# Shifting the tokens of a short convolution: two DMAs of 127 rows in place of four of 112 and 15

## The reference

```python
def short_conv_mixer(x_in, b_g, c_g, p):
    u = c_g * x_in
    up = jnp.pad(u, ((0, 0), (1, 1), (0, 0)))
    w = p['conv_w']
    y = up[:, :-2] * w[0] + up[:, 1:-1] * w[1] + up[:, 2:] * w[2] + p['conv_b']
    return b_g * y

x = x + gate1 * (jnp.concatenate([o_a, o_b, o_c, o_d], axis=-1) @ p['w_out'])
```

## Time and profile before

| | before |
|---|---|
| median of 3 runs | 5456.26 us (5455.68 to 5457.26) |
| the profiled execution | 5455.68 us, its span 5453.9 us |
| busy share of the span | PE 60%, DVE 69%, POOL 51%, PEld 32%, ACT 12% |
| hardware DMA queue (SyncE's) | 69332 packets, 7.3% of the 16 DMA engines |
| software DMA queue (the experts) | 368640 packets, 62.2% |

### The profile page before, as it was taken

How to read it: one execution, slowest core, us unless ns; L and a number is a source line. 1 busy time by engine, 2 the same in 40 slices (tenths; PEclk the granted TensorE clock), 3 DMA queues, 4 the chain that set the end, 5 groups by cost and what they waited for, 6 DMA issues and landing times. The chain is left out here.

```text
span 5453.9 us, 39401 instructions
## 1 busy us (share of the span) xinstructions
PE 3258.3 (60%) x12134; PEld 1731.0 (32%) x12134; DVE 3782.4 (69%) x7387; ACT 657.4 (12%) x1592; POOL 2758.7 (51%) x2848
## 2 busy tenths in 40 slices
PE   7988888893507145071479787699470541705326
PEld 1467725551202011020134676465220110202102
DVE  1046565379798897988630565736989979799784
ACT  0012122111101000010110121311010100101001
POOL 0012230157777777777730222303677777777775
PEclk9989988997859678595799899699795875958769
DMA  7100042199999999999961000007999999999999
GB/s 265 51 4 2 1 151 68 70 351 397 410 409 404 409 399 408 403 404 409 402 261 51 5 1 18 16 32 258 397 409 410 405 408 397 409 409 398 409 402 365
DMA packets 438180, 1483.20 MB, mean 272 GB/s; under 512 B 47514, under 2 KB 54802, under 8 KB 436306
## 3 DMA queue, kind: packets, MB, share of 16 engines
q0 software_dynamic: 368640, 1342.34, 62.2%
q1 hardware_dynamic: 69332, 138.35, 7.3%
HBM read 1466.17 MB, written 11.73 MB: 271 GB/s over the span
## 5 line engine op out<-in xcount | busy, mean ns | idle before, releaser
L1741 PE MATMUL ps<-z,o 128*128 128x512 f32 x2560 | 1261.4, 621 | 705.2 <-DMA z<-in_peer_v,experts 353.2
L1773 DVE CUSTOM_DVE_ANT_0 z<-z,ps 128x1024 f32<-128x1024 f32 x1280 | 1530.3, 1216 | 64.5 <-DMA z<-in_peer_u,experts 26.7
L1596 POOL DMA_INDIRECT z<-in_peer_u,experts x1280 | 1211.4, 946 | 569.0 <-DVE state L1773 252.1
L1596 POOL DMA_INDIRECT z<-in_peer_v,experts x1280 | 1211.0, 946 | 464.1 <-issue 303.4
L1798 DVE SCALAR_TENSOR_TENSOR ps<-z,state,ps 128x1024 f32<-128x1024 f32 x630 | 808.4, 1283 | 395.7 <-DMA z<-in_peer_v,experts 395.1
L1741 PEld LDWEIGHTS ps<-z,o 128*128 128x128 f32 x2560 | 451.3, 194 | 1510.4 <-ACT o L1654 931.7
L1669 PE MATMUL ps<-const,hT 128*128 128x128 f32 x80 | 17.8, 396 | 1163.2 <-ACT o L1654 1163.2
L1669 PEld LDWEIGHTS ps<-const,hT 128*128 128x128 f32 x80 | 14.4, 207 | 1168.5 <-ACT o L1654 1014.8
L1654 ACT ACTIVATE o<-const,state 128x128 f32<-128x128 f32 x640 | 244.3, 398 | 1068.2 <-PE ps L1741 1063.6
L431 PE MATMUL ps<-w,hT 128*128 128x512 f32 (+1 forms) x960 | 365.6, 543 | 1.8 <-DVE hT L401 1.8
L679 POOL TENSOR_TENSOR kn<-kn,neg_half 128x4 f32<-128x4 f32 x20 | 20.1, 1007 | 482.8 <-DVE kn L717 399.5
(11 more groups left out here) (363 smaller groups left out, 4682.6 us busy)
## 6 DMA issues: line engine op xcount, KB each, us to landing
w<-in_w_mod SPq DMA_DIRECT2D x12, 2048.0 KB, 8.0
gate<-in_w_mod SPq DMA_DIRECT2D x96, 256.0 KB, 3.0
w<-in_w_in SPq DMA_DIRECT2D x10, 2048.0 KB, 8.0
z<-in_peer_u,experts POOLq DMA_INDIRECT x1280, 13.4
z<-in_peer_v,experts POOLq DMA_INDIRECT x1280, 12.1
w<-in_peer_wq SPq DMA_DIRECT2D x8, 2048.0 KB, 12.6
w<-in_w_out SPq DMA_DIRECT2D x4, 2048.0 KB, 11.3
scores<-rows SPq DMA_DIRECT2D x8, 1024.0 KB, 8.8
```

What stands on the lines that cost most here:

```text
L1596: eng.indirect_dma_start(m.ring[j % RING], None, at_layer_rows(table), bass.IndirectOffsetOnAxis(ap=m.experts[:, t % 2, k:k + 1], axis=0)) ...
L1741: mm = eng.matmul(m.ps[:, 4 + n, :], m.diag[:, (done + q) % DIAGS, :], row_j[:, n * 512:(n + 1) * 512], start=(q == 0), stop=(q == SLOTS / ...
L1773: eng.tensor_tensor_reduce(row_j, row_j, h_rows, 1.0, 0.0, ALU.mult, ALU.add, m.acts[:, k:k + 1]).then_inc(used_v, 1)
```

## The change

Each shift is one DMA of 127 rows where there were two, of 112 and of 15. The two small ones stay. The order on SyncE changes a little, and the waits count four DMAs and not six.

```diff
-                for a, b in ((0, 112), (112, P - 1)):
-                    eng.dma_start(before[a + 1:b + 1, :, :], u[a:b, :, :]).then_inc(shifted, 16)
-                    eng.dma_start(after[a:b, :, :], u[a + 1:b + 1, :, :]).then_inc(shifted, 16)
+                eng.dma_start(before[1:P, :, :], u[0:P - 1, :, :]).then_inc(shifted, 16)
                 eng.dma_start(before[0:1, 2:TILES, :], u[P - 1:P, 1:TILES - 1, :]).then_inc(shifted, 16)
+                eng.dma_start(after[0:P - 1, :, :], u[1:P, :, :]).then_inc(shifted, 16)
                 eng.dma_start(after[P - 1:P, 1:TILES - 1, :], u[0:1, 2:TILES, :]).then_inc(shifted, 16)
...
-                eng.wait_ge(shifted, 96)
+                eng.wait_ge(shifted, 64)
...
-                        eng.wait_ge(shifted, 96)
+                        eng.wait_ge(shifted, 64)
```

## The result

The changed kernel takes 5526.09 us (median of 4 runs, 5523.89 to 5530.31) beside 5456.76 us for the one before (4 runs, 5455.68 to 5457.94): 69.3 us or 1.3% slower, ratio 1.0131, 95% interval 1.0118 to 1.0142. The spans are 5522.6 and 5453.9 us, 68.7 apart. The forecast was 5539 with a range of 5515 to 5608.

A forecast was written before the change was run, and what follows sets the result against it. Most of the span was put in the expert stages, at 400 to 410 GB/s, with the shifts hidden. Delays of 38.2 (second layer) and 45.3 us (first) make 83.5; 5455.7 + 83.5 = 5539 us, range 5515 to 5608.

The forecast's parts named there:

- One engine for 127 rows: Shifts: engines get equal shares, so 127 rows run on one; the other reading, rows counted up to 16, gives 16.
- 48 ns a piece, 61.0 us: Shifts: 1270 pieces of 1 KB through one engine at 48 ns each take 61.0 us, against about 6 before.
- Second layer, a wait at GpSimd less 5.6 us of slack: GpSimd's first convolution instruction waits 43.9 us; idle time before the keys' root absorbs 5.6, leaving 38.2 us.
- First layer, the wait at TensorE's piece 4, nothing at GpSimd: Weight loads queue behind the shifts, so TensorE waits 43.3 us for piece 4; GpSimd then finds its data there.
- The clock, 2 us: First layer: after idling, TensorE's work behind the stall may restart at clock 0.50; 0 to 5 us, taken as 2.
- First layer, 45.3 us: First layer's whole cost: TensorE's wait of 43.3 us for piece 4 plus 2 us for the clock.
- The sum, 83.5: Whole kernel: 38.2 us for the second layer plus 45.3 for the first, 83.5 us slower.
- All 16 engines: Rival: 127 rows spread over 16 engines in shares of 7 and 8, still hidden; 5455.5 us, chance 0.07.
- One slow engine: Rival: a lone engine also takes 74 ns a piece, so the transfer takes 94.5 us; 5606 us, chance 0.15.
- Loads not held back: Rival: the engine turns to weight loads between pieces, first layer pays at GpSimd alone; 66.1 us, 5522 total, chance 0.08.

The follow-up runs named there:

- the experiment with ScalarE: Kernel before, with one shift as a single 127-row DMA issued from ScalarE's queue and not SyncE's: 5805.06 beside 5792.76 us, ratio 1.0026.

## Why the prediction was right, step by step

**One engine for 127 rows**: right, by the 8 small packets. The rule was open between two readings; 126, 121 and 118 rows, with 14, 11 and 2 engines, settle it for the largest divisor up to 16, on SyncE's queue.

**48 ns a piece, 61.0 us**: a little too high. The first convolution instruction of the second layer could go at 3491.61, and the first DMA was issued at 3434.74. With 1.3 us for the start and 0.5 for the end, as the prediction took them, 55.1 us are left for 1270 pieces, 43.4 ns each, between the 40 of the experts' stream and the quietest shared row of 51. That is 5.9 us less a layer. It is nearly all of what the forecast was too slow in the second layer (38.2 forecast, 32.0 arrived at VectorE). A part of it is the reckoning: the prediction multiplied by the busy share, 1.05 in its rows, and by that same reckoning the lone engine shows 0.066 x 16 x 56.2 us / 1276 = 46 ns, though it is through with a piece every 43. That the shared pieces' longer time comes from the ports, as the prediction has it, no run here shows; they show 62 ns beside 46 by the same reckoning.

**Second layer, a wait at GpSimd less 5.6 us of slack**: right as a mechanism: 37.58 - 5.6 = 32.0, and VectorE shows 32.19.

**First layer, the wait at TensorE's piece 4, nothing at GpSimd**: right. The prediction had the loads issued in time and standing behind the pieces in the engine's queue. In fact, the greater part is a wait one step earlier: SyncE itself was held until 752.05, 34 us after its time, and of the rest, 7.0 us from there to 759.06, some 3 are what a load takes anyway (3.0 us to landing). Only the other 4 are the order in the engine's queue, behind the last pieces: between 752.1 and 759 the queues move up to 368 GB/s until some 757, and then 24, the rate of one engine, whose shares of these loads come last. Since SyncE is let go about 5 us before the engine is through with its pieces, both ways end at about the same time, so the forecast of this wait did not suffer; that is luck as far as the mechanism goes. By the prediction's mechanism SyncE would be free to do something else in these 34 us, and it was not.

**The clock, 2 us**: the granted clock behind the stall was 0.50, as feared. Two windows of the changed kernel, columns as in the earlier trace rows:

```profile
760.00:762.00 2.00, 2.00 (x5) 0.83 (x4) 0.00 (x0) 0.00 (x0) 0.00 (x0) 0.50 0.09 12
762.00:764.00 2.00, 2.00 (x12) 1.09 (x11) 0.42 (x1) 0.00 (x0) 0.00 (x0) 0.94 0.42 125
```

Piece 4's products took 1.86 us there and not 1.02, the gate's 1.22 and not 0.70. VectorE's L1180 came 39.7 us late (762.12 against 722.39) with 38.2 us of longer waiting, so 1.5 us for the slower products. The 2 of the forecast were about right.

**First layer, 45.3 us**: 34.6 by the start of the second layer's stage, 36.9 in `stage_mix` itself. The delay at VectorE's L1180 was 39.7 us, 5.6 less than forecast, of which the pieces' time is the greater part. The other 5 are what was given back between 762 us and the second layer, for which the prediction had no term. Some 2 us of it are the clock again, with the other sign. TensorE in the second tile, before (granted 0.50 there) and after (1.00):

```profile
739.28 1.65 PE L1057 MATMUL ps<-gate,latT 64*128 64x384 f32 x2
740.86 2.07 PE L1058 MATMUL ps<-gate,latT 128*128 128x512 f32 x2
```

```profile
778.66 0.91 PE L1056 MATMUL ps<-gate,latT 64*128 64x384 f32 x2
779.50 1.12 PE L1057 MATMUL ps<-gate,latT 128*128 128x512 f32 x2
```

In the kernel before the clock fell to 1.2 GHz in this place; with everything later it did not. These products took the delay from 39.9 to 37.7 us, and in the second run of the changed kernel and in the one with the first layer alone changed they were fast as well (1.13 us for the longer one). What sets the place at which the clock falls was not tried.

The rest lies behind the stage. By SyncE's first loads, the attention took 109.5 us before and 108.4 after, the output projection 82.1 and 80.6: 2.7 us less. In the second layer the same two went the other way, from 108.6 to 109.6 and from 79.8 to 81.4: 2.7 more. So the two cancel in the sum, which the forecast, with nothing for either, owes to luck. They need not come from the delay: with 126 and 1 rows, where nothing is late, the second layer's projection took 84.2 us.

**The sum, 83.5**: measured 69.3. The term that was mis-sized is the time of a piece, with 5.9 us too many in each layer, and the term that was missing is the 2 to 3 us that the first layer's stage gave back.

**The rivals.** All 16 engines: refuted. One slow engine: refuted, 43 ns. Loads not held back: refuted for one queue, by the wait at TensorE; for two queues the experiment with ScalarE shows the engine taking turns, so this rival was right in its mechanism and wrong in its place. The time alone would not have refuted it: 69.3 us measured are nearer to its 66.1 than to the 83.5 of the forecast, and only the place of the wait, at TensorE and not at GpSimd, decides.

## What to carry to other kernels

Before merging or cutting a DMA, factor the number of its rows. In every transfer counted here on SyncE's queue the number of engines was the largest divisor of the rows up to 16; a prime above 16, as 127, means one engine, with 24 GB/s here. A transfer that is hidden has a deadline, and costs only what it ends later than that: read the deadline at whoever waits first, and look also at what is issued behind it on the same queue, since the first to suffer may be a load that has nothing to do with it. It is cheap to check in a profile: small packets, one for each engine and transfer, and the DMA share, near 1 for all engines and 0.06 for one.

## What the runs showed of the hardware

- The issue of a DMA to one engine costs 0.8 us at once, but the next DMA on that queue then takes 23.3 and 26.3 us to issue, even one of three pieces. It is as if the queue accepted only so many pieces ahead: SyncE was free again about 5 us, some 110 to 120 pieces, before the transfers' end. Behind 118 rows, on two engines, the next DMAs took 9.26 and 12.42 us. The 1.70 and 1.45 us of the 15-row DMAs before, behind those of 112 rows, may be the same thing in small.
- One DMA engine moves 1 KB pieces within SBUF in 43 to 44 ns when it is alone, 23 to 24 GB/s. By busy share, 16 together took 62 ns a piece, and one alone 46.
- GpSimd's queue also put 127 rows on one engine, and held GpSimd until the first transfer was over. A VectorE instruction on 128x4 numbers took 5.16 us while GpSimd worked at the first of these DMAs; in the kernel before the same instruction takes 0.17 to 0.43 (L1161 there, ten times).
- While GpSimd stood still, VectorE was faster. Before, GpSimd ran a multiplication of 0.72 us from 3422.36 beside this one; after, it was waiting. The same instruction of the second layer, L817 on 128x192, before and after:

```profile
3422.53 0.77 DVE L817 TENSOR_TENSOR o<-gate,const 128x192 f32<-128x192 f32 x1
```

```profile
3456.03 0.36 DVE L817 TENSOR_TENSOR o<-gate,const 128x192 f32<-128x192 f32 x1
```
